# Two-layer mixer backbone on one core: latents' norms filled with gate products, norm sums reordered, unread products behind two broadcasts

## The chip, the cores and the metric

The kernel runs on one core of one Trainium2 chip. The metric is device time in microseconds (us) of one execution, the median of several. PE is TensorE (matrix products), DVE is VectorE, ACT is ScalarE, POOL is GpSimd; SP issues DMAs.

## The reference

Two layers work on 256 latent tokens and 256 context tokens of width 1024, in fp32. What matters of a layer:

```python
ux = rmsnorm(h, g_pre_mix[l]) * (1 + sc1x) + sh1x
yx, yc = token_mixers(ux, uc, ...)
h = h + ga1x * rmsnorm(yx, g_post_mix[l])
ux = rmsnorm(h, g_pre_ffn[l]) * (1 + sc2x) + sh2x
h = h + ga2x * rmsnorm(swiglu(ux, w_ffn_in[l], w_ffn_out[l]), g_post_ffn[l])

# in token_mixers: the latents of branch A, then four attention branches and their gates
q = heads(rmsnorm(p['a_cq'], g_a_q) @ w_a_uq, H_A)
kv = heads(rmsnorm(p['a_ckv'], g_a_kv) @ w_a_ukv, H_A)
up = jnp.einsum('btnw,nwd->btnd', o, w_branch)
g = jax.nn.sigmoid(gate_pre.reshape(up.shape))
return jnp.sum(g * up, axis=2) @ w_out
```

Branch A has 8 heads with low-rank queries and keys; B, C and D have 8 heads each in 4 pairs. Context tokens go through the same layer, except in the last one, where they only give keys and values.

## The kernel before

Activations stand with channels on partitions and tokens along the row, 512 columns in layer 0 and 256 for most of layer 1. Every fp32 product is made of three fp32r products (`three`: high x high, high x low, low x high), so each weight piece of 512 columns is first split: ACT copies the high part (L1323), DVE (L1508) or POOL (L1283) subtracts it to get the low part. A piece of four weight tiles gives 12 products on PE.

The order of all work is written out as a list of steps by `build_plan`, and every engine walks this list in order. There is no scheduler at run time: an engine that waits for a semaphore holds up everything behind it in its own queue. A layer has these stages.

1. The first projection (`group`, step `gmm`, 96 products in 8 pieces) makes the latents `ckv`, `cq` (two tiles) and the rotary key `kr` while `apply` still norms the input tile by tile (DVE L1632, ACT L1364 and L1369, DVE L1638 for the low part).
2. The latents' norms: `evac` and `evacsq` copy and square a product out of PSUM (ACT L1378, L1382), `stat` sums squares over partitions (PE L1864), then DVE, POOL and DVE make the reciprocal root and write it wide (`wide`, DVE L1584), `bcast` turns it over the partitions (PE L1923), `gn` multiplies (DVE L1654), `qks` stores high and low parts (ACT L1386, DVE L1673). `rot` and `rope` rotate `kr`. Then come the first head's projections and gates 0 and 1 (four pieces of 12 products).
3. Attention in slots. A slot (`run_slot`) has the scores of one item (`sc`, `sc2`), the row maximum (`mx`), the exponential (`ex`), the transposes (`tr`, PE L2002) and the value product (`pv`) of earlier items. Between them stand the projection steps of the next unit (a head of A, a pair of B, C or D), which `spread_over` deals out to the unit's slots, and filler: gate and up products of 12 products a piece, which `levels` and `Filler` spread by their cost. A unit's chain is: products, `evac`, for D also `stat` and `gain` (`bcast`, `gn`), `rotate` (PE L1932, then POOL and DVE), `store` (`qks`). The next unit's scores wait for that store.
4. `output` makes eight tiles of y; after each one ACT scales it into Y (`yev`, L1351), and squares y, Y and the product of Y with the residual are summed for the norms (`ysq`, `zsq`, `hz`, and the adds `yadd`, `zadd`, `hadd` on POOL, L1251).
5. `turnover` goes from one block to the next: the sums over partitions on PE (`sums` L1882 and L1886, `sums_rest` L1894), the first norm's root and broadcast, the `moment` of the new residual from the sums, its root and a second broadcast (both PE L1923), then `post` adds the normed y to the residual (DVE L1646, L1648) and `apply` feeds the next group of products. There are three turnovers, and a shorter end after the last block.

The lines that deal the projection steps out to slots, and the order in `apply`, are:

```python
for c, make in micro:
    at = min(slots - 1, int((gone + c / 2) * slots / whole))
    out[at].append((c, make))
    gone += c
```

```python
fill.todo = gate(0, 0) + gate(1, 0)
```

Of the kernel before, what the change touches and what calls it, by code (L numbers as in the profile page):

```python
# [29 lines left out]
P = 128  # L30
# [22 lines left out]
MOD_US = 1.2  # L53
AHEAD = 4
# [7 lines left out]
for _n, _w in (('ident', 128), ('ones', 1), ('power', 8), ('rotB', 128), ('rotA', 128), ('cosB', 256), ('sinB', 256),  # L62
# [21 lines left out]
RINGS = {'acc': 3, 'raw': 3, 'tmp': 2, 'fil': 2, 'gate': 8, 'Q': 2, 'K': 2, 'V': 2, 'S': 2, 'P': 2, 'Pn': 2, 'T': 1,  # L84
# [11 lines left out]
    'wide': ('stat_wide',), 'moment': ('moment_part', 'moment_part', 'moment_part', 'moment_part', 'moment_ready'),  # L96
# [12 lines left out]
    'tout': ('out_turned', 'out_copied'),  # L109
# [126 lines left out]
def build_plan():  # L236
# [28 lines left out]
    def apply(nm, l, which, n, first, posts=None):  # L265


        posts = posts or {}
        for kt in range(KT + 1):
            if kt < KT:  # L270
                p.take('tmp', ('ap', nm, kt), ('ap_full', (nm, kt)))
                p.take('fil', ('ap', nm, kt), ('ap_lo', (nm, kt)))
                p.step('apA', (nm, kt), l=l, which=which, n=n)
                for step in posts.get(kt, ()):
                    step()
            if kt:
                p.step('apB', (nm, kt - 1), n=n)
                p.step('gmm', (first, kt - 1))
# [4 lines left out]
    def turnover(nmo, nm, l, which, n, first):  # L283


        p.step('sums', nmo, n=n, what=('ysq', 'hz', 'zsq'))
# [4 lines left out]
        p.step('bcast', nmo, n=n)  # L291
        p.step('moment', nm, n=n)
# [3 lines left out]
        p.step('bcast', nm, n=n)  # L296
        post(nmo, 0, n)
# [25 lines left out]
    for l in range(DEPTH):  # L323
# [22 lines left out]


        for k, n in ((ckv, NTOK), (cq[0], nq), (cq[1], nq)):
            p.take('raw', k, ('op_hi', k), ('op_lo', k))
            p.take('fil', k, ('stat_sum', ckv if k == ckv else cq[1]))  # L350
            p.step('evac', k, rows=(0, P), n=n)
            p.step('evacsq', k, rows=(0, P), n=n)
            if k == ckv:
                norm_stat(ckv, [ckv], 1, KVL, NTOK, [('normed', ckv)])
                p.step('gn', ckv, bc=ckv, n=NTOK, g=(l, 82))
                p.step('qks', ckv, src='raw', rows=(0, P), n=NTOK, dst=('ckv', 0))
        norm_stat(cq[1], cq, 1, QL, nq, [('normed', cq[1])])
        p.take('raw', kr, ('op_hi', kr), ('op_lo', kr))
        p.step('evac', kr, rows=(0, DA), n=NTOK)
        for t, k in enumerate(cq):  # L360
            p.step('gn', k, bc=cq[1], n=nq, g=(l, 80 + t))
            p.step('qks', k, src='raw', rows=(0, P), n=nq, dst=('cq', t))
        p.take('acc', ('rot', kr), ('rope_sin', kr))
        p.step('rot', kr, rows=DA, t='A', normed=False)
        p.take('tmp', ('rope', kr), ('roped', kr))
        p.step('rope', kr, rows=DA, t='A')
        p.step('qks', kr, src='raw', rows=(NOPE, DA), n=NTOK, dst=('kr', 0))
# [90 lines left out]
        def projection(u):  # L458
# [41 lines left out]
            return [k0, k1, k_raw, q0, k_sum, q1, q_raw, k_norm, v0, q_sum, k_rot, v1, v_raw, q_norm, k_store, v_turn,  # L500
# [189 lines left out]
        fill.todo = gate(0, 0) + gate(1, 0)  # L690
# [20 lines left out]
        for n in range(4):  # L711
            a, b = n * per + 3 if n else 0, (n + 1) * per + 3
            if n == 0:
                fill.todo += [step for dt in range(2, KT) for step in gate(dt, 0)]
# [20 lines left out]
        def output(nmo, l, which, pieces_of, src, kts, need, ends=False):  # L735
# [3 lines left out]
            for dt in range(KT):  # L739
# [10 lines left out]
                p.step('yev', key, n=nq, l=l, which=which)  # L750
                for what in whats:
# [4 lines left out]
                    p.step(what, key, n=nq)  # L756
                for what in whats if 0 < dt < KT - 1 else ():
                    p.step(what[0] + 'add', key, n=nq)
# [50 lines left out]
    p.step('sums', nmf, n=SEQ, what=('ysq',))  # L809
    p.step('mstat', nmf, nh=1, dim=D, n=SEQ, after=('first_sums', nmf))  # L810
    p.step('wide', nmf, n=SEQ, of=1)
    p.take('bc', ('bc', nmf), ('post_scaled', (nmf, KT - 1)))
    p.step('bcast', nmf, n=SEQ)
    for kt in range(KT):
        post(nmf, kt, SEQ)
# [44 lines left out]
def build(nc, x, c, ctx, c_ctx, w_mod, b_mod, g_pre_mix, g_post_mix, g_pre_ffn, g_post_ffn, w_in, g_a_q, g_a_kv,  # L860
# [26 lines left out]
    with ExitStack() as es:  # L887
# [102 lines left out]
        def raw(key):  # L990
            at = RAW_AT + plan.slot['raw', key] * NTOK
            return Y[:, at:at + NTOK]
# [213 lines left out]
        def _(pool):  # L1206
            for kind, key, f in steps:
# [28 lines left out]
                elif kind == 'pow':  # L1236
                    m = f['n'] // P
                    pool.wait_ge(sem['moment_ready'], count['moment_ready', key])
                    pool.tensor_tensor(stat[:, 4, 0:m], stat[:, 3, 0:m], const('power')[:, 0:m],
                                       ALU.pow).then_inc(sem['stat_rstd'], 1)  # L1240
                elif kind in ('yadd', 'zadd', 'hadd'):
# [3 lines left out]
                    what, done = {'yadd': ('ysq', 'y_added'), 'zadd': ('zsq', 'z_added'), 'hadd': ('hz', 'h_added')}[kind]  # L1245
# [59 lines left out]
        def _(act):  # L1305
            for kind, key, f in steps:
# [63 lines left out]
                elif kind in ('evac', 'evacsq'):  # L1370
# [4 lines left out]
                    if kind == 'evac':  # L1375
                        for name, k_ in plan.freed['raw', key]:
# [93 lines left out]
        def _(dve):  # L1470
            for kind, key, f in steps:
# [92 lines left out]
                elif kind in ('stat', 'mstat'):  # L1564
# [10 lines left out]
                    if key == (0, 'pre_mix'):  # L1575
                        dve.tensor_copy(stat[:, 5, 0:m], sums[:, 0:m])
# [16 lines left out]
                elif kind == 'moment':  # L1593
# [4 lines left out]
                    done = count['moment_part', key] - 4  # L1598
# [6 lines left out]
                    dve.tensor_tensor(a, a, r, ALU.mult).then_inc(sem['moment_part'], 1)  # L1605
                    dve.wait_ge(sem['moment_part'], done + 3)
                    dve.tensor_tensor(h2, h2, a, ALU.add).then_inc(sem['moment_part'], 1)
# [503 lines left out]
```

## Time and profile before

| what | value |
|---|---|
| median of 3 runs | 1996.81 us (1995.76 to 1998.09) |
| the profiled execution | 1997.45 us |
| its span, first to last instruction | 1995.6 us |
| PE busy | 1832.3 us (92%) |
| DVE busy | 1222.5 us (61%) |
| ACT busy | 885.5 us (44%) |
| POOL busy | 681.6 us (34%) |
| mean granted PE clock | 0.961 |

The granted clock is 1.00 at 2.4 GHz and 0.50 at 1.2 GHz. Busy time of PE therefore holds time in which it worked at half pace; a stretch is read with its busy time and its granted clock together.

### The profile page before, as it was taken

What the parts mean: (1) busy time and instruction counts of PE and PEld (TensorE: products, weight loads), DVE (VectorE), ACT (ScalarE), POOL (GpSimd) and SP (SyncE); (2) the same over time, 40 slices, a digit from 0 to 9 for tenths busy, and PEclk for the clock granted to TensorE, in tenths of its full rate; (3) what the DMA queues carried; (4) which work ended last, traced back from release to release, by engine and by line L of the source; (5) the groups of instructions that cost most, each with busy time, mean ns of one, the idle gap of its engine ahead of it and who ended that gap; (6) DMA issues with size and microseconds to landing.
All of it is one profiled execution on the core that took longest, in us unless ns stands there. A gap on an engine that the chain in (4) does not pass through costs nothing. (4 is left out here: it accounts for less than half of the span.)

```text
span 1995.6 us, 31796 instructions
## 1 busy us (share of the span) xinstructions
PE 1832.3 (92%) x10675; PEld 1579.9 (79%) x10675; DVE 1222.5 (61%) x2381; ACT 885.5 (44%) x1918; POOL 681.6 (34%) x615
## 2 busy tenths in 40 slices
PE   7788899999998889989999999878999998989998
PEld 7666677778777768778888878767888887879997
DVE  6335565667775664667777775646554456776654
ACT  2435544444443444453222233456555544555453
POOL 6134434445443443541111112225335534351100
PEclk9979999999999999979999999789999999989998
DMA  7111223334433322424546664122343433436664
GB/s 292 55 37 43 60 78 87 85 107 121 116 96 85 80 64 68 134 83 134 148 140 186 198 197 118 46 57 66 97 110 97 117 91 89 113 117 175 185 180 122
DMA packets 381804, 223.15 MB, mean 112 GB/s; under 512 B 51607, under 2 KB 377549, under 8 KB 380621
## 3 DMA queue, kind: packets, MB, share of 16 engines
q1 hardware_dynamic: 379340, 217.97, 38.5%
q10 hardware_dynamic: 2304, 3.15, 0.6%
q8 instruction: 89, 1.46, 0.3%
q14 instruction: 71, 0.57, 0.1%
HBM read 217.92 MB, written 3.15 MB: 111 GB/s over the span
## 5 line engine op out<-in xcount | busy, mean ns | idle before, releaser
L1778 PE MATMUL bank<-Uhi,w_ring 128*128 128x512 f32 (+2 forms) x1664 | 592.5, 356 | 24.3 <-DVE Ulo L1638 15.6
L1780 PE MATMUL bank<-Uhi,w_ring 128*128 128x512 f32 (+2 forms) x1664 | 578.0, 347 | 0.0
L1779 PE MATMUL bank<-Ulo,w_ring 128*128 128x512 f32 (+2 forms) x1664 | 577.7, 347 | 0.0
L1508 DVE TENSOR_TENSOR w_ring<-load_ring,w_ring 128x512 fp32r<-128x512 f32 (+2 forms) x432 | 339.0, 802 | 173.2 <-ACT w_ring L1323 148.3
L1323 ACT ACTIVATE w_ring<-load_ring 128x512 fp32r<-128x512 f32 (+4 forms) x640 | 369.1, 602 | 90.9 <-PE bank L1780 70.3
L1778 PEld LDWEIGHTS bank<-Uhi,w_ring 128*128 128x128 f32 (+1 forms) x1664 | 319.8, 192 | 69.2 <-issue 22.4
L1780 PEld LDWEIGHTS bank<-Uhi,w_ring 128*128 128x128 f32 (+1 forms) x1664 | 319.0, 192 | 40.5
L1283 POOL TENSOR_TENSOR w_ring<-load_ring,w_ring 128x512 fp32r<-128x512 f32 (+3 forms) x208 | 249.2, 1201 | 290.6 <-issue 143.6
L1779 PEld LDWEIGHTS bank<-Ulo,w_ring 128*128 128x128 f32 (+1 forms) x1664 | 320.1, 192 | 34.9
L1778 PE MATMUL bank<-Z,w_ring 128*128 128x512 f32 (+2 forms) x784 | 273.7, 349 | 16.2 <-DVE Z L1673 6.1
L1779 PE MATMUL bank<-Z,w_ring 128*128 128x512 f32 (+2 forms) x784 | 269.1, 343 | 0.0
L1780 PE MATMUL bank<-Z,w_ring 128*128 128x512 f32 (+2 forms) x784 | 268.9, 343 | 0.0
L1271 POOL TENSOR_TENSOR Y<-Y,small 128x512 f32<-128x512 f32 x160 | 166.6, 1041 | 238.6 <-DVE small L1724 215.6
L1418 ACT ACTIVATE Y<-bank,small 128x512 f32<-128x512 f32 (+1 forms) x192 | 117.2, 612 | 146.2 <-DVE small L1707 145.9
L1778 PEld LDWEIGHTS bank<-Z,w_ring 128*128 128x128 f32 (+1 forms) x784 | 151.0, 193 | 36.6 <-issue 9.1
L1729 DVE TENSOR_TENSOR Z<-bank,Z 128x512 fp32r<-128x512 f32 x160 | 109.4, 684 | 99.7 <-ACT Z L1426 99.1
L1780 PEld LDWEIGHTS bank<-Z,w_ring 128*128 128x128 f32 (+1 forms) x784 | 151.1, 193 | 17.6
L1779 PEld LDWEIGHTS bank<-Z,w_ring 128*128 128x128 f32 (+1 forms) x784 | 151.3, 193 | 16.2 <-issue 0.3
L1300 POOL TENSOR_TENSOR Z<-fil,Z 128x512 fp32r<-128x512 f32 (+1 forms) x44 | 44.6, 1016 | 320.7 <-ACT Z L1460 320.7
L1778 PE MATMUL bank<-Z 128*64 128x256 f32 (+2 forms) x368 | 111.3, 303 | 25.1 <-DVE Z L1673 15.5
L1426 ACT ACTIVATE Z<-bank 128x512 fp32r<-128x512 f32 x160 | 95.0, 594 | 81.9 <-PE bank L2002 79.6
L1529 DVE SCALAR_TENSOR_TENSOR mod_sums<-mod_place,sc,mod_sums 128x256 f32<-128x256 f32 x224 | 123.6, 592 | 3.4 <-issue 0.3
(138 smaller groups left out, 2402.9 us busy)
## 6 DMA issues: line engine op xcount, KB each, us to landing
load_ring<-in_w_in SPq DMA_DIRECT2D x192, 256.0 KB, 3.0
load_ring<-in_w_ffn_in SPq DMA_DIRECT2D x160, 256.0 KB, 3.1
mod_ring<-in_w_mod SPq DMA_DIRECT2D x96, 256.0 KB, 3.1
load_ring<-in_w_ffn_out SPq DMA_DIRECT2D x80, 256.0 KB, 3.3
mod_place<-in_w_mod SPq DMA_DIRECT2D x64, 256.0 KB, 2.8
load_ring<-in_w_branch SPq DMA_DIRECT2D x64, 256.0 KB, 2.8
mod_w<-in_w_mod SPq DMA_DIRECT2D x8, 1024.0 KB, 13.6
load_ring<-in_w_in SPq DMA_DIRECT2D x64, 128.0 KB, 2.6
```

Source lines behind the costliest of these rows:

```text
L1271: pool.tensor_tensor(prob('Pn', key).rearrange("p (m k) -> p m k", m=m), prob('P', key).rearrange("p (m k) -> p m k", m=m), small[:, plan. ...
L1283: pool.tensor_tensor(w_ring[:, slot, 1, 0:sz], load_ring[:, plan.slot['load', key], 0:sz], w_ring[:, slot, 0, 0:sz].bitcast(F32), ALU.subt ...
L1300: pool.tensor_tensor(operand('hid', 1, key[1], n), fil[:, plan.slot['fil', ('ffn', key)], 0:n], operand('hid', 0, key[1], n).bitcast(F32), ...
L1323: act.activation(w_ring[:, plan.slot['w', key], 0, 0:sz], load_ring[:, plan.slot['load', key], 0:sz], ACT.Copy).then_inc(sem['w_hi'], 1)
L1418: ins = act.activation(prob('P', key)[:, a:b], s_bank(key)[:, a:b], ACT.Exp, bias=sm[:, 2 + i:3 + i], scale=scale_of(key), accum_out=sm[:, ...
L1426: act.activation(dst, src, ACT.Copy).then_inc(sem['pt_hi'], 1)
L1508: dve.tensor_tensor(w_ring[:, slot, 1, 0:sz], load_ring[:, plan.slot['load', key], 0:sz], w_ring[:, slot, 0, 0:sz].bitcast(F32), ALU.subtr ...
L1529: ins = dve.scalar_tensor_tensor(out=a, in0=w, scalar=by, in1=a, op0=ALU.mult, op1=ALU.add)
L1729: dve.tensor_tensor(dst, src, hi.bitcast(F32), ALU.subtract).then_inc(sem['pt_lo'], 1)
L1778: pe.matmul(dst, lhs[0], rhs[0], start=start, stop=False)
L1779: pe.matmul(dst, lhs[0], rhs[1], start=False, stop=False)
L1780: return pe.matmul(dst, lhs[1], rhs[0], start=False, stop=stop)
```

## The change

Five edits stand in the diff.

- Latents: the gates are put into the latents' norms. `AT_START` takes three gates (layer 0) or four (layer 1) instead of two, and of their six or eight pieces four or six are placed one at a time between the `stat`, `bcast` and `rot` steps. The evacuation of `kr` comes first and goes to a place of its own (`rawk`), so that the bank in which gates are made is free.
- Slots: `spread_over` gets fixed places for chains of five steps (B) and seven steps (D), and puts the others half a slot earlier; the order in D's first unit is altered.
- Sums: the last tile is squared before it is scaled (`ysq` before `yev`), `sums` holds only what the first norm needs, the rest goes to `sums_rest`; `hadd` moves from POOL to DVE; `moment` has four operations instead of five.
- `warm`: products of two constant tiles into bank 6, which nobody reads: four behind the first broadcast and six behind the second at each turnover, and four and four at the end. 38 in all.
- `apply`: the third `post` comes behind the first tile's products, not ahead of its low part, and so on for each tile.

```diff
+AT_START = (3, 4)
...
-        for kt in range(KT + 1):
-            if kt < KT:
-                p.take('tmp', ('ap', nm, kt), ('ap_full', (nm, kt)))
-                p.take('fil', ('ap', nm, kt), ('ap_lo', (nm, kt)))
-                p.step('apA', (nm, kt), l=l, which=which, n=n)
-                for step in posts.get(kt, ()):
-                    step()
-            if kt:
-                p.step('apB', (nm, kt - 1), n=n)
-                p.step('gmm', (first, kt - 1))
+        scaled(0)
+        for step in posts.get(0, ()):
+            step()
+        for kt in range(KT):
+            if kt + 1 < KT:
+                scaled(kt + 1)
+            p.step('apB', (nm, kt), n=n)
+            p.step('gmm', (first, kt))
+            for step in posts.get(kt + 1, ()):
+                step()
...
-        p.step('sums', nmo, n=n, what=('ysq', 'hz', 'zsq'))
+        p.step('sums', nmo, n=n)
         p.step('sums_rest', nmo, n=n, what=('hz', 'zsq'))
...
         p.step('bcast', nmo, n=n)
+        p.step('warm', nmo, times=4)
         p.step('moment', nm, n=n)
...
         p.step('bcast', nm, n=n)
+        p.step('warm', nm, times=6)
...
-            for c, make in micro:
-                at = min(slots - 1, int((gone + c / 2) * slots / whole))
-                out[at].append((c, make))
+            places = {5: (0, .3, .3, .6, .7), 7: (0, .2, .2, .4, .55, .75, .8)}.get(len(micro))
+            for i, (c, make) in enumerate(micro):
+                at = places[i] * slots if places else (gone + c / 2) * (slots - .5) / whole
+                out[min(slots - 1, int(at))].append((c, make))
                 gone += c
...
-        fill.todo = gate(0, 0) + gate(1, 0)
+        fill.todo = [step for dt in range(AT_START[l]) for step in gate(dt, 0)]
...
+        latent(ckv, NTOK)
+        p.take('rawk', kr, ('op_hi', kr), ('op_lo', kr))
+        p.step('evac', kr, rows=(0, DA), n=NTOK)
+        latent_sum(ckv, [ckv], KVL, NTOK)
+        latent(cq[0], nq)
+        fill.piece()
+        latent_rstd(ckv, NTOK)
+        latent(cq[1], nq)
+        latent_sum(cq[1], cq, QL, nq)
+        latent_store(ckv, ckv, NTOK, 82, ('ckv', 0))
+        fill.piece()
+        latent_rstd(cq[1], nq)
+        p.take('acc', ('rot', kr), ('rope_sin', kr))
+        p.step('rot', kr, rows=DA, t='A', normed=False)
+        fill.flush()
+        fill.piece()
+        if l:
+            fill.piece()
+            fill.flush()
+        for t, k in enumerate(cq):
+            latent_store(k, cq[1], nq, 80 + t, ('cq', t))
...
+        fill.piece()
+        if l:
+            fill.piece()
+        fill.flush()
...
+                elif kind == 'warm':
+
+                    for _ in range(f['times']):
+                        pe.matmul(bank[6][:, :], ident_r[:, :], mask_r[:, :], start=True, stop=True)
```

The order of PE's instructions behind the first group of layer 0, before. In all rows of this kind `bank` is PSUM, `C` the constants, `fil` the squares, `wide` the roots written wide, `Uhi` and `Ulo` the normed input, `Z` the attention's store, `w_ring` split weights; x4 is four in a row.

```order
L1864 MATMUL bank<-C,fil 128x1 x4
L1923 MATMUL bank<-C,wide 128x128 x4
L1864 MATMUL bank<-C,fil 128x1 x8
L1923 MATMUL bank<-C,wide 128x128 x4
L1932 MATMUL bank<-Y,C 96x256
L1778 MATMUL bank<-Z,w_ring 96x512
```

Now, from the end of the first gate piece (the row with L1828) on:

```order
L1828 MATMUL bank<-Uhi,w_ring 128x512
L1979 MATMUL bank<-C,wide 128x128 x4
L1912 MATMUL bank<-C,fil 128x1 x8
L1826 MATMUL bank<-Uhi,w_ring 128x512
L1827 MATMUL bank<-Ulo,w_ring 128x512
L1828 MATMUL bank<-Uhi,w_ring 128x512
```

A gate piece (12 products, of which one or three rows are shown) now stands behind the first sums and behind the second ones; two more follow the rotation of `kr`, ahead of the first head's products.

PE at the end of unit D0 of layer 0, before: the rotation (L1932) of unit D1's queries stands with only one item's transposes (L2002) between it and the scores (L1981) that need them.

```order
L1780 MATMUL bank<-Z 64x256
L1932 MATMUL bank<-Y,C 128x256
L2002 MATMUL bank<-C,Y 128x128 x4
L1981 MATMUL bank<-Z 128x512 x6
L1778 MATMUL bank<-Uhi,w_ring 128x512
```

Now, on PE at the end of the same unit: the rotation (L1988) follows the scores of the context item (L2037), and 50 rows stand between it and the next unit's scores.

```order
L1828 MATMUL bank<-Z,w_ring 128x512
L2058 MATMUL bank<-C,Y 128x128 x4
L2037 MATMUL bank<-Z 128x256 x12
L1988 MATMUL bank<-Y,C 128x256
L1826 MATMUL bank<-Z,w_ring 128x512
L1827 MATMUL bank<-Z,w_ring 128x512
```

So the rotation has moved ahead by filler products and by the scores of a whole item.

DVE at the turnover between the blocks of layer 0, before. L1646 and L1648 are a `post`, L1632 scales a tile, L1638 makes its low part `Ulo`, for which PE waits.

```order
L1632 TENSOR_TENSOR tmp<-H,bank 128x512
L1646 TENSOR_TENSOR Y<-Y,bank 128x512
L1648 TENSOR_TENSOR H<-H,Y 128x512
L1632 TENSOR_TENSOR tmp<-H,bank 128x512
L1646 TENSOR_TENSOR Y<-Y,bank 128x512
L1648 TENSOR_TENSOR H<-H,Y 128x512
L1638 TENSOR_TENSOR Ulo<-fil,Uhi 128x512
```

Now, on DVE at the same turnover:

```order
L1680 TENSOR_TENSOR tmp<-H,bank 128x512
L1694 TENSOR_TENSOR Y<-Y,bank 128x512
L1696 TENSOR_TENSOR H<-H,Y 128x512
L1680 TENSOR_TENSOR tmp<-H,bank 128x512
L1686 TENSOR_TENSOR Ulo<-fil,Uhi 128x512
L1694 TENSOR_TENSOR Y<-Y,bank 128x512
L1696 TENSOR_TENSOR H<-H,Y 128x512
```

The low part (L1686) has moved ahead of the second `post` pair (L1694, L1696).

## Rows read from the trace of the kernel before

**Rows 1.** The page, part 1: busy time of each engine, share of the span, instructions.

```profile
PE 1832.3 (92%) x10675; PEld 1579.9 (79%) x10675; DVE 1222.5 (61%) x2381; ACT 885.5 (44%) x1918; POOL 681.6 (34%) x615
```

**Rows 2.** Windows: stretch, its us, busy PE, PEld, DVE, ACT, POOL, granted clock, DMA share, GB/s.

```profile
90.00:129.50 39.50, 26.34 (x105) 21.43 (x106) 10.39 (x19) 12.35 (x24) 9.84 (x10) 0.70 0.10 26
129.50:250.00 120.50, 104.04 (x546) 83.04 (x546) 65.54 (x151) 68.05 (x162) 51.49 (x55) 0.93 0.20 50
580.00:780.00 200.00, 179.97 (x1001) 147.56 (x1001) 122.68 (x266) 82.14 (x189) 89.91 (x77) 0.96 0.28 76
862.00:864.80 2.80, 2.80 (x26) 2.76 (x25) 1.12 (x1) 2.36 (x5) 1.86 (x2) 1.00 0.00 0
862.20:904.30 42.10, 36.07 (x161) 31.09 (x160) 27.36 (x47) 20.68 (x37) 8.08 (x7) 0.76 0.30 88
865.00:885.30 20.30, 14.27 (x53) 12.58 (x53) 14.00 (x28) 7.10 (x13) 3.21 (x3) 0.50 0.33 101
904.30:1262.00 357.70, 353.65 (x1617) 293.50 (x1617) 248.21 (x461) 108.34 (x200) 57.46 (x41) 1.00 0.53 158
1300.60:1328.10 27.50, 16.97 (x92) 15.16 (x92) 11.78 (x23) 10.30 (x24) 4.31 (x6) 0.69 0.13 33
1328.10:1395.00 66.90, 60.05 (x398) 49.63 (x397) 44.23 (x107) 47.90 (x115) 31.73 (x37) 1.00 0.28 67
1600.00:1715.00 115.00, 103.51 (x771) 94.58 (x770) 69.62 (x153) 57.90 (x130) 45.34 (x47) 0.97 0.34 86
```

**Rows 3.** Timeline of PE, latents of layer 0: start us, us, instruction [idle before, releaser].

```profile
91.26 1.02 PE L1864 MATMUL bank<-C,fil 128*128 128x1 f32 x8 [1.27 <-ACT fil L1382]
94.18 2.05 PE L1923 MATMUL bank<-C,wide 128*128 128x128 f32 x8 [1.90 <-DVE wide L1584]
99.77 3.54 PE L1864 MATMUL bank<-C,fil 128*128 128x1 f32 x16 [3.54 <-ACT fil L1382]
105.21 2.04 PE L1923 MATMUL bank<-C,wide 128*128 128x128 f32 x8 [1.89 <-DVE wide L1584]
...
111.71 0.71 PE L1778 MATMUL bank<-Z,w_ring 128*96 128x512 f32 x1 [3.61 <-DVE Z L1673]
```

**Rows 4.** Timeline of PE: successive products of 512 columns at either clock.

```profile
112.22 0.63 PE L1779 MATMUL bank<-Z,w_ring 128*96 128x512 f32 x1
112.65 0.63 PE L1780 MATMUL bank<-Z,w_ring 128*96 128x512 f32 x1
...
126.14 0.39 PE L1778 MATMUL bank<-Uhi,w_ring 128*128 128x512 f32 x1
126.37 0.39 PE L1779 MATMUL bank<-Ulo,w_ring 128*128 128x512 f32 x1
```

**Rows 5.** Waits of PE, 129.5 to 250 us (branch A): us, times, longest us.

```profile
PE bank L1778 <- DVE Z L1673: 10.9, 7, 2.7
PE bank L1932 <- ACT Y L1378: 5.4, 7, 1.1
```

**Rows 6.** Waits of PE, 250 to 415 us (branch B).

```profile
PE bank L1932 <- ACT Y L1378: 3.8, 3, 1.3
```

**Rows 7.** Waits of PE, 415 to 580 us (branch C).

```profile
PE bank L1778 <- DVE Z L1729: 8.3, 5, 3.1
```

**Rows 8.** Waits of PE, layer 1, 1395 to 1600 us (branches B and C).

```profile
PE bank L1932 <- ACT Y L1378: 3.2, 3, 1.1
```

**Rows 9.** Timeline of PE, turnover inside layer 0.

```profile
869.77 2.05 PE L1923 MATMUL bank<-C,wide 128*128 128x128 f32 x8
872.60 2.05 PE L1923 MATMUL bank<-C,wide 128*128 128x128 f32 x8 [0.77 <-DVE wide L1591]
879.90 0.76 PE L1778 MATMUL bank<-Uhi,w_ring 128*128 128x512 f32 x1 [5.26 <-DVE Ulo L1638]
```

**Rows 10.** Timeline of DVE, the same turnover.

```profile
877.53 0.68 DVE L1646 TENSOR_TENSOR Y<-Y,bank 128x512 f32<-128x512 f32 x1
878.25 0.69 DVE L1648 TENSOR_TENSOR H<-H,Y 128x512 f32<-128x512 f32 x1
```

More of the change, by code:

```diff
@@ L713, in build_plan @@
             if n == 0:
-                fill.todo += [step for dt in range(2, KT) for step in gate(dt, 0)]
+                fill.todo += [step for dt in range(AT_START[l], KT) for step in gate(dt, 0)]
             else:
@@ L756, in output @@
                     p.step(what, key, n=nq)
+                    if dt == KT - 1 and what == 'ysq':
+                        p.step('yev', key, n=nq, l=l, which=which)
                 for what in whats if 0 < dt < KT - 1 else ():
@@ L808, in build_plan @@
                {j: [('hid_lo', (l, min(4 * j + 3, FT - 1)))] for j in range(-(-FT // 4))}, ends=last)
-    p.step('sums', nmf, n=SEQ, what=('ysq',))
+    p.step('sums', nmf, n=SEQ)
     p.step('mstat', nmf, nh=1, dim=D, n=SEQ, after=('first_sums', nmf))
+    p.step('warm', (nmf, 0), times=4)
     p.step('wide', nmf, n=SEQ, of=1)
@@ L813, in build_plan @@
     p.step('bcast', nmf, n=SEQ)
+    p.step('warm', (nmf, 1), times=4)
     for kt in range(KT):
@@ L1621, in _ @@
                                       ALU.mult).then_inc(sem['hz_done'], 1)
+                elif kind == 'hadd':
+                    nm, dt = key
+                    n = f['n']
+                    dve.wait_ge(sem['hz_done'], count['hz_done', key])
+                    if dt > 1:
+                        dve.wait_ge(sem['h_added'], count['h_added', (nm, dt - 1)])
+                    a = sum_place('hz', (nm, 0))[:, 0:n]
+                    dve.tensor_tensor(a, a, sum_place('hz', key)[:, 0:n], ALU.add).then_inc(sem['h_added'], 1)
                 elif kind == 'apA':
@@ L1876, in _ @@
                 elif kind == 'sums':
-                    for j, what in enumerate(f['what']):
-                        done = {'ysq': 'y_added', 'hz': 'h_added', 'zsq': 'z_added'}[what]
-                        pe.wait_ge(sem[done], count[done, (key, KT - 2)])
-                        for tt in range(f['n'] // P):
-                            pe.matmul(sums_at(j, tt), sum_place(what, (key, 0))[:, tt * P:(tt + 1) * P], const('ones'),
-                                      start=j < 2 and tt == 0, stop=False, skip_group_check=True)
+                    pe.wait_ge(sem['y_added'], count['y_added', (key, KT - 2)])
+                    for tt in range(f['n'] // P):
+                        pe.matmul(sums_at(0, tt), sum_place('ysq', (key, 0))[:, tt * P:(tt + 1) * P], const('ones'),
+                                  start=tt == 0, stop=False, skip_group_check=True)
                     pe.wait_ge(sem['ysq_done'], count['ysq_done', (key, KT - 1)])
@@ L1888, in _ @@
                     ins.then_inc(sem['first_sums'], 1)
+                elif kind == 'warm':
+                    for _ in range(f['times']):
+                        pe.matmul(bank[6][:, :], ident_r[:, :], mask_r[:, :], start=True, stop=True)
                 elif kind == 'sums_rest':
+                    for j, what in enumerate(f['what']):
+                        done = what[0] + '_added'
+                        pe.wait_ge(sem[done], count[done, (key, KT - 2)])
+                        for tt in range(f['n'] // P):
+                            pe.matmul(sums_at(1 + j, tt), sum_place(what, (key, 0))[:, tt * P:(tt + 1) * P], const('ones'),
+                                      start=j == 0 and tt == 0, stop=False, skip_group_check=True)
                     for j, what in enumerate(f['what']):
```

74 lines of the change are left out of this document (38 added, 36 removed).

## The prediction

> **What bounds the kernel now.** The engines' busy times come first: PE 1832.3 us of a span of 1995.6, DVE far behind at 61% [rows 1]. So a change pays in one of two ways: it takes away some of PE's 163 us without work (1995.6 - 1832.3), or it gives back pace that PE lost at the low clock. The mean clock of 0.961 puts that at 0.039 x 1995.6 = 78 us at most. Second, the windows by stage say where both lie [rows 2]. The output and ffn stages are all but full (353.65 of 357.70 us, clock 1.00) and have nothing to give. The latents have 13 us of idle in 39.5, at clock 0.70; branch A of layer 0 16.5 us at 0.93; branch D 20 us at 0.96; the turnover 6 us at 0.76. Third, the timeline and the waits say what ends the idle there: a chain through ACT, DVE and POOL, with nothing ready behind it in PE's own queue [rows 3, 5, 9]. Does the order of the queue put work of the right length there, and is that work ready?
>
> I count savings against the profiled execution, 1997.45 us (0.6 above the median).
>
> **Latents, layer 0: 16.5.** Two rows of products start 0.43 us apart at the low clock and 0.23 at the high one [rows 4], so a piece of 12 takes 2.7 us at the high clock (12 x 0.227) and 5.1 at the low. Before, 39.5 us held four pieces [rows 2]. In the change it holds six. Its length, if PE never waits long: six pieces 16.4; sums 1.0 and, at the high clock, half of 3.54 (taken as 2.0); two broadcasts of 2.05, of which I take 1.25 each, between half and the whole; rotations and turning of v 1.6; the first head's nine products 2.1; the wait of 1.3 ahead of the first sums, which nothing fills [rows 3]. That is 27. The two added pieces were paid later before, at 5.5, so the saving is 39.5 + 5.5 - 27 = 18. The cover fits: the first piece starts about 92.3 and would end at 95.0, where the first broadcast could start at 94.18; after the second broadcast the first head's operands need 4.4 us (107.25 to 111.71) [rows 3], and two pieces are 5.5. I take 1.5 off for one low-clock spell more, leaving 16.5. Bounds: nothing of the clock comes back (13 us of idle only, less 2), 11; all of it, 18.
>
> **Latents, layer 1: 11.5.** Gate pieces have half the columns there, so 1.4 us each. Eight instead of four stand in a stretch of 27.5 with 10.5 of idle at clock 0.69 [rows 2]. The same working gives 20.2 us with the four added ones (5.5): 27.5 + 5.5 - 20.2 = 12.8, less 1.3. Bounds 7 and 13.
>
> **Turnovers: 4.7.** In the first, PE's first product waits 5.26 us for the low part [rows 9], and a `post` pair of about 0.7 and 0.7, paced at 1.3, stands ahead of it on DVE [rows 10]; the change puts it behind. The shorter `moment` saves a little more. Against it, the four unread products run at the low clock, 4 x 0.43 = 1.7 us, where PE had only 0.77 us free: the second broadcast goes out some 0.9 late. The six behind it (2.6) lie in the 5.26. The product thus starts about 0.9 earlier. The group behind it runs at the low clock until 885.3 [rows 2]; if the unread products raise it by the time it starts, twelve products cost 2.7 us instead of 5.1. I take 2.5 in all; ends -0.9 and 3.5. The other two turnovers get 0.8 and 0.7, as DVE's chain paces them whatever PE does, and the end 0.7. The moved sums are worth nothing: the same 48 products stand ahead of the first broadcast. `hadd` on DVE costs nothing, because DVE is idle for 110 of 358 us in the output and ffn stages [rows 2]; without that cover it would add 0.7 a tile.
>
> **Attention slots: 43.** I take idle first. Branch A, layer 0: 16.5 us idle [rows 2], of it 10.9 for the store of the next head and 5.4 for the copy ahead of the rotation [rows 5]. Half a slot earlier moves the store out of the way, but the rotation's copy now queues on ACT behind the exponential: 4 net. Branch B: three rotations wait 3.8 [rows 6], and the fixed places put scores between; 3.8, and 3.2 in layer 1 [rows 8]. Branch D, layer 0: 20 us [rows 2], since copy, rotation and store all stand in the unit's last slot; the order shows 50 rows between rotation and scores now, and I take 14.5. Branch A, layer 1: 5.5 of 6.85; branch D, layer 1: 7.5 of 11.5 [rows 2]. Sum 38.5. The clock gives more: PE's busy time in these stretches would shrink by 104.04 x 0.07 = 7.3, 179.97 x 0.04 = 7.2 and 103.51 x 0.03 = 3.1 if it never fell [rows 2]. The spells stand where PE idles; I take half of the first and 80% of the others, 11.9 in all. Off the 50.4 I take 15%, since each unit's products moved ahead also leave work further back bare: branch C, whose chain is unfilled in places, waits 8.3 us for the stores of values [rows 7]. That leaves 43. Bounds: 15 and 55.
>
> The Trainium skill ("TensorE: Matmul & The Clock Gate", section "What's actually happening") says that the clock's ramp costs under 1% of a typical span and need not be modelled. By it the clock's part of all savings would be capped near 20 us; the measured mean of 0.961 says 3.9% here, so rows are followed.
>
> **Sum.** 16.5 + 11.5 + 4.7 + 43 = 75.7; 1997.45 - 75.7 = 1921.75, and 0.6 less for the median: **1921**.
>
> **Rivals.**
> - The slots only move waits (0.13). A wait on the store is exchanged for one on the copy or on values, as [rows 7] shows it where chains are spread evenly. Against it: D's chain is so bunched that any spreading helps. The slots then give 0: 1997.5 - 32.7 = 1964 or so.
> - The pieces in the latents come too late (0.07): their weights must be split by ACT and DVE, which also carry the norms' chain; PE waits for them in place of the root. Half of the 28 goes: 1935.
> - The clock stays up from the latents to the end (0.08). With the long idle gone no gap falls in attention or the turnovers, and the terms that I halved come whole: another 10 us, 1911. For it: most low spells follow idle time. Against it: the clock fell at 864.9, right behind 2.80 us in which PE was busy all the time, and stayed at 0.50 to 885.3 [rows 2].
> - It gets slower (0.04). Place: branch A of both layers. With products dealt half a slot earlier its last slots have only small products and waits for the copy, and the clock falls there. At half clock the 164 us of busy time in the two branches (104.04 + 60.05, [rows 2]) double. The 16.5 + 6.85 = 23 us of idle there absorb a part, so if all of it runs low the loss is 141, against 75.7 saved: 2062. It decides from more than half of that time at the low clock.
>
> [...]
>
> **How the numbers follow.** The forecast has 0.68, the rivals 0.13, 0.07, 0.08 and 0.04. The forecast's own range is 1903 to 1938, from the bounds of the terms taken together and not all at one end (all at their low ends would save about 11 + 7 + 1 + 15 = 34, all at the high ends 18 + 13 + 6 + 55 = 92). The range for 8 in 10 must reach into the first rival without holding it whole: 1900 to 1957. Measurements of this kernel tell changes of about 0.2%, 4 us, from none. Faster by more has the forecast and three rivals, 0.96, less 0.01 for cases close to none: 0.95; within, 0.01; slower, 0.04.
>
> **What would show it.** Right: the stretch from the first group to the first scores falls from 39.5 to about 27 us with 72 gate products in it, at a clock over 0.85; the wait of the products for the store (10.9 in branch A) halves; branch D is idle for 5 to 8 us instead of 20; the first product of the turnover's group waits near 3.5 us instead of 5.26 and the low spell there is shorter. Wrong: branch A's waits for the copy above 15 us; DVE or ACT named before the latents' pieces; the low spell from 864.9 as long as before; the mean clock still under 0.97. The whole fails if PE's idle time stays above 130 us.

## The result, and the profile after

The changed kernel takes 1984.5 us, median of 6 runs (1980.31 to 1995.71), against 1997.33 us (1995.76 to 1998.41) for the kernel before: a ratio of 0.9947, interval 0.9926 to 0.9968. It is faster by 12.8 us at the medians, where 76 were forecast, and the time lies outside the range. Its profiled execution took 1985.07 us. Its six runs lie 15 us apart; the granted clock of the slowest is 0.966, of the others 0.969 to 0.972.

The page of the changed kernel, part 1 (against [rows 1]):

```profile
PE 1834.7 (93%) x10713; PEld 1584.7 (80%) x10713; DVE 1229.0 (62%) x2396; ACT 883.0 (45%) x1918; POOL 654.7 (33%) x597
```

PE has the same work and the 38 unread products, and the span fell by 12.3 us to 1983.3: its idle time went from 163 to 149 us.

Windows of the changed kernel at the stages of [rows 2], in the same columns; the bounds are placed by the same instructions: latents, A, D, turnover, output and ffn of layer 0; then latents, A, B with C, and D of layer 1.

```profile
90.00:118.40 28.40, 26.00 (x134) 20.75 (x132) 10.77 (x18) 13.01 (x26) 11.01 (x12) 1.00 0.18 46
118.40:240.60 122.20, 104.14 (x547) 84.56 (x546) 63.10 (x152) 67.66 (x162) 50.95 (x55) 0.92 0.20 50
564.90:753.50 188.60, 172.91 (x977) 142.34 (x977) 124.67 (x263) 78.56 (x182) 87.75 (x76) 0.96 0.28 76
837.40:882.00 44.60, 38.84 (x172) 32.79 (x171) 26.26 (x46) 20.56 (x37) 7.77 (x6) 0.85 0.27 83
882.00:1239.60 357.60, 353.55 (x1619) 293.44 (x1617) 250.94 (x467) 108.33 (x200) 48.21 (x35) 1.00 0.53 158
1282.50:1307.70 25.20, 18.75 (x141) 17.13 (x141) 12.37 (x25) 12.87 (x32) 6.01 (x8) 1.00 0.25 60
1307.70:1379.30 71.60, 59.38 (x359) 49.81 (x360) 41.93 (x104) 45.41 (x110) 30.35 (x37) 0.93 0.22 52
1379.30:1594.00 214.70, 199.97 (x1360) 178.04 (x1359) 105.37 (x239) 107.13 (x243) 89.87 (x83) 0.98 0.40 100
1593.80:1705.60 111.80, 103.01 (x782) 94.05 (x781) 69.40 (x154) 58.91 (x132) 46.95 (x47) 0.98 0.36 90
```

Four things stand in them. The latents of layer 0 are close to the forecast's 27: 39.5 has become 28.4 at clock 1.00, with two more pieces in it. Branch A got longer in both layers (120.5 to 122.2, 66.9 to 71.6), and so did B with C in layer 1: 214.7 us, and before, in the same columns:

```profile
1395.00:1600.00 205.00, 196.89 (x1371) 175.10 (x1370) 106.25 (x238) 107.64 (x245) 90.25 (x83) 1.00 0.42 106
```

The turnover inside layer 0 is 2.5 us longer than before, though the low spell is shorter. The output and ffn stages didn't move, with `hadd` on DVE (x461 to x467): that was free.

### The profile page after: what moved, and what is told of

Its sections match the earlier page's. It is cut to its first block and busy times, and to the rows that moved or that the text cites. A ratio compares the mean times of both kernels' runs of the same rounds, so it can differ in the third digit from the quotient of the medians.

```text
span 1983.3 us, 31864 instructions
## 1 busy us (share of the span) xinstructions
PE 1834.7 (93%) x10713; PEld 1584.7 (80%) x10713; DVE 1229.0 (62%) x2396; ACT 883.0 (45%) x1918; POOL 654.7 (33%) x597
## 3 DMA queue, kind: packets, MB, share of 16 engines
q1 hardware_dynamic: 379340, 217.97, 38.6%
## 5 line engine op out<-in xcount | busy, mean ns | idle before, releaser
L1828 PE MATMUL bank<-Uhi,w_ring 128*128 128x512 f32 (+2 forms) x1664 | 577.7, 347 | 0.0
L1550 DVE TENSOR_TENSOR w_ring<-load_ring,w_ring 128x512 fp32r<-128x512 f32 (+2 forms) x432 | 333.2, 789 | 163.8 <-ACT w_ring L1365 133.1
L1828 PEld LDWEIGHTS bank<-Uhi,w_ring 128*128 128x128 f32 (+1 forms) x1664 | 319.2, 192 | 40.5
L1828 PE MATMUL bank<-Z,w_ring 128*128 128x512 f32 (+2 forms) x784 | 267.7, 341 | 0.0
L1460 ACT ACTIVATE Y<-bank,small 128x512 f32<-128x512 f32 (+1 forms) x192 | 117.3, 613 | 173.2 <-DVE small L1755 173.2
L1828 PEld LDWEIGHTS bank<-Z,w_ring 128*128 128x128 f32 (+1 forms) x784 | 150.4, 192 | 17.2
L1826 PE MATMUL bank<-Z 128*64 128x256 f32 (+2 forms) x368 | 113.3, 308 | 21.4 <-DVE Z L1777 10.9
```

Of the source, the lines that this page charges most:

```text
L1460: ins = act.activation(prob('P', key)[:, a:b], s_bank(key)[:, a:b], ACT.Exp, bias=sm[:, 2 + i:3 + i], scale=scale_of(key), accum_out=sm[:, ...
L1550: dve.tensor_tensor(w_ring[:, slot, 1, 0:sz], load_ring[:, plan.slot['load', key], 0:sz], w_ring[:, slot, 0, 0:sz].bitcast(F32), ALU.subtr ...
L1826: pe.matmul(dst, lhs[0], rhs[0], start=start, stop=False)
L1828: return pe.matmul(dst, lhs[1], rhs[0], start=False, stop=stop)
```

## Where the time went in the trace

The timeline of PE, latents of layer 0, changed kernel (the rows between are gate products):

```profile
92.35 1.02 PE L1912 MATMUL bank<-C,fil 128*128 128x1 f32 x8 [1.26 <-ACT fil L1424]
...
96.36 1.13 PE L1979 MATMUL bank<-C,wide 128*128 128x128 f32 x8
97.33 1.84 PE L1912 MATMUL bank<-C,fil 128*128 128x1 f32 x16
...
101.88 1.05 PE L1979 MATMUL bank<-C,wide 128*128 128x128 f32 x8
```

The waits of 1.90, 3.54 and 1.89 of [rows 3] are gone, and the sixteen sums (3.54 to 1.84 us) and the broadcasts (2.05 to 1.13 and 1.05) take half as long.

The waits of PE in branch A of layer 0 (118.4 to 240.6 us), changed kernel: us, times, longest us.

```profile
PE bank L1988 <- ACT Y L1420: 8.2, 4, 2.2
PE bank L1826 <- DVE Z L1721: 5.3, 5, 1.8
PE bank L2058 <- POOL Y L1313: 4.6, 2, 2.3
```

Against [rows 5] the wait for the store has halved, from 10.9 to 5.3, and the copy ahead of the rotation has grown from 5.4 to 8.2; a third wait of 4.6 is new, of transposes for the probabilities that POOL scales. 16.3 us of waits have become 18.1: this is the first rival (waits are only moved), in this branch.

The timeline of PE, turnover inside layer 0, changed kernel; L1938 are the unread products:

```profile
845.71 2.05 PE L1979 MATMUL bank<-C,wide 128*128 128x128 f32 x8
847.42 2.05 PE L1938 MATMUL bank<-mask_r,ident_r 128*128 128x512 f32 x4
849.27 1.32 PE L1979 MATMUL bank<-C,wide 128*128 128x128 f32 x8
850.35 1.63 PE L1938 MATMUL bank<-mask_r,ident_r 128*128 128x512 f32 x6
854.43 0.48 PE L1826 MATMUL bank<-Uhi,w_ring 128*128 128x512 f32 x1 [2.45 <-DVE Ulo L1686]
...
861.67 0.50 PE L1826 MATMUL bank<-Uhi,w_ring 128*128 128x512 f32 x1 [1.50 <-DVE Ulo L1686]
...
869.22 0.50 PE L1826 MATMUL bank<-Uhi,w_ring 128*128 128x512 f32 x1 [1.81 <-DVE Ulo L1686]
```

The clock is up at the first product, as hoped, and the wait ahead of it fell from 5.26 to 2.45. But PE now waits again and again inside the group. The timeline of DVE there says why:

```profile
855.91 0.69 DVE L1686 TENSOR_TENSOR Ulo<-fil,Uhi 128x512 fp32r<-128x512 f32 x1
858.40 0.69 DVE L1550 TENSOR_TENSOR w_ring<-load_ring,w_ring 128x512 fp32r<-128x512 f32 x1 [1.80 <-issue]
859.01 0.68 DVE L1694 TENSOR_TENSOR Y<-Y,bank 128x512 f32<-128x512 f32 x1
859.73 0.69 DVE L1696 TENSOR_TENSOR H<-H,Y 128x512 f32<-128x512 f32 x1
```

Behind the low part stands the split of the next weight piece (L1550), and DVE idles 1.8 us ahead of it. The row names no releaser ("issue"); the timeline of ACT has the copy of the high part, which the split subtracts, ending just before, at 858.32:

```profile
857.70 0.62 ACT L1365 ACTIVATE w_ring<-load_ring 128x512 fp32r<-128x512 f32 x1
```

Only then does DVE do the `post`, which could have covered part of that wait. Over the whole group DVE waits 8.2 us ahead of such splits (854 to 882 us); before it was 6.2 (879.9 to 904.5), so the old order covered a part and not all. I measured each turnover from its first sum on PE to the end of the 96th and last product of the group. Before, the first product stands 17.7, 18.1 and 12.0 us behind the first sum and the 96th ends at 42.3, 38.6 and 28.0. After, the first stands at 17.0, 16.8 and 10.5 and the 96th ends at 44.6, 42.9 and 28.4. So the change wins 3.5 us at the first product and is 7.1 behind at the end of the groups.

## The experiments

Each kernel ran 4 to 12 times. The ratio is that to the kernel before in the same job, with its interval; the kernel before read 1997.1 to 1998.0 in all of them.

| run | us | ratio | interval |
|---|---|---|---|
| the changed kernel | 1984.50 | 0.9947 | 0.9926 to 0.9968 |
| e1_apply_undone | 1982.04 | 0.9918 | 0.9902 to 0.9934 |
| e2_slots_undone | 1989.01 | 0.9959 | 0.9944 to 0.9974 |
| e3_latents_undone | 2008.38 | 1.0047 | 1.0030 to 1.0064 |
| e4_no_unread | 1991.80 | 0.9964 | 0.9950 to 0.9978 |
| e5_places_only | 1959.00 | 0.9815 | 0.9797 to 0.9833 |
| e6_post_first | 1984.74 | 0.9942 | 0.9927 to 0.9958 |
| e7_places_post_first | 1950.63 | 0.9778 | 0.9760 to 0.9796 |
| e8_places_alone | 1975.86 | 0.9900 | 0.9883 to 0.9917 |
| e9b_latents_alone | 1986.95 | 0.9957 | 0.9942 to 0.9971 |
| e10b_half_slot_in_c | 1977.02 | 0.9897 | 0.9881 to 0.9912 |
| e11b_places_no_unread | 1964.26 | 0.9835 | 0.9819 to 0.9852 |
| e12b_places_old_apply | 1958.60 | 0.9806 | 0.9792 to 0.9821 |

**One part undone.** e1_apply_undone has the old order in `apply`:

```diff
-            p.step('gmm', (first, kt))
-            for step in posts.get(kt + 1, ()):
-                step()
...
+                for step in posts.get(kt, ()):
+                    step()
+            if kt:
+                p.step('apB', (nm, kt - 1), n=n)
+                p.step('gmm', (first, kt - 1))
```

> The changed kernel with the old order in apply (each post ahead of the low part again), all else kept. Theory: behind the new order DVE meets the split of a weight piece with nothing left to do and idles 1.8 us for ACT's high part, at five tiles, then still has the post to do; the groups behind the turnovers are longer by 3 and 5.7 us in the traces (order of work aligned). Undone, the time falls by 5 to 10 us, to about 1977, although the first product waits longer. Rival, the forecast's own term: the new order saves 2.5 to 4 us, and undone the time rises to 1987 to 1989.

The direction is the theory's: undoing it is no loss, and the 96th product ends at 42.0, 37.7 and 27.3. The medians differ by 2.5 us, the ratios by 5.8, and the two intervals overlap, so the size isn't settled by this run. In its trace DVE waits 5.1 us ahead of the splits of the first group, against 8.2.

e2_slots_undone has the spread of before, and the old order in D's first unit:

```diff
-            places = {5: (0, .3, .3, .6, .7), 7: (0, .2, .2, .4, .55, .75, .8)}.get(len(micro))
...
+                at = min(slots - 1, int((gone + c / 2) * slots / whole))
```

> The changed kernel with the old spread over the slots (no fixed places, no half slot earlier, old order in D's first unit). Theory: branches B and D gain some 10 + 9 us in layer 0 and 3 + 9 in layer 1 by the fixed places, branches A and C lose 2 + 5 and 6 + 14 by the half slot earlier: net almost nothing, 1980 to 1995 us. Rival, the forecast's term of 43: about 2025 us.

1989.0: by the medians all edits of the slots together are worth 4.5 us here, by the ratios 2.4, with overlapping intervals, where the forecast had 43. This is the term that failed.

e3_latents_undone has the old block for the latents and `gate(0, 0) + gate(1, 0)` at the start:

```diff
-        fill.todo = [step for dt in range(AT_START[l]) for step in gate(dt, 0)]
+        fill.todo = gate(0, 0) + gate(1, 0)
...
```

> The changed kernel with the old latents (two gates at the start, norms unfilled). Theory: the added pieces came out of branch A, where they had covered waits, so that part of the gain is given back: latents 17 + 9 us, less 5 to 6 in each layer's branch A, leaving 12 to 16: 1997 to 2001 us. Rival, the forecast's term of 28 is whole: 2012 us.

2008.4: the latents are worth 24 us inside the change by the medians (20 by the ratios), nearer to the forecast's 28 than to my 12 to 16. Without them the rest of the change is slower than the kernel before.

e4_no_unread leaves out the four `warm` steps:

```diff
-        p.step('warm', nmo, times=4)
...
-        p.step('warm', nm, times=6)
...
```

> The changed kernel without the 38 unread products. Theory: they cut the low-clock spell at a turnover from 20.5 to 10.2 us, but the group behind is paced by DVE with the new apply order, so little of it reaches the time: 1984 to 1990 us. Rival 1, the clock is worth it all the same (about 5 us at each of two turnovers): 1993 or more. Rival 2, they only delay the second broadcast by 0.8 us each: 1982.

7.3 us slower at the medians, a value between theory and rival, but 3.4 by the ratios, and the two intervals overlap: the size isn't settled. The second rival, that they cost time, finds no support. The traces don't put the gain at the turnovers. The low spell behind the first broadcast is 20.5 us long again instead of 10.2, yet the group takes 27.1 us, with the unread products 27.6. And most of the difference between the traces can't be put down to them. Up to the first turnover the two kernels are the same, instruction for instruction, and this trace is already 5.1 us behind there, of 7.2 in all; 3.8 of them stand in branch C of layer 0, where the low clock holds for 20.5 us instead of 10.2. Behind that point the latents of layer 1 take 1.7 us more and branch C 2.3, and the turnovers 1.8 less.

**The slots taken apart.** e5_places_only keeps the fixed places of B's and D's chains and takes the half slot back from all the others:

```diff
-                at = places[i] * slots if places else (gone + c / 2) * (slots - .5) / whole
+                at = places[i] * slots if places else (gone + c / 2) * slots / whole
```

> The changed kernel with the fixed places of B's and D's chains kept, and all other chains (those of A and C) spread as before, without the half slot. Theory: the half slot is what loses. By the aligned traces branch C loses 5 us in layer 0 and 14 in layer 1 by it, and branch A a few: 1960 to 1968 us. Rival, the clock: what one stage gains another loses to spells of the low clock that move about, and the time stays within 5 us of the changed kernel's 1984.5.

1959.0, just below the theory's 1960 to 1968, and the intervals are far apart: **the half slot costs 25 us**. Against e2, whose slots are all as before, the fixed places and the order in D's first unit are worth 30 us inside the change (29 by the ratios). e10b_half_slot_in_c puts it back for C alone:

```diff
-                at = places[i] * slots if places else (gone + c / 2) * (slots - .5) / whole
+                at = places[i] * slots if places else (gone + c / 2) * (slots - early) / whole
...
-                micros[at_item:at_item + len(mine)] = spread_over(micro, len(mine))
+                micros[at_item:at_item + len(mine)] = spread_over(micro, len(mine), .5 * (u2[1] == 'C'))
```

> The kernel with places only, with the half slot put back for branch C's chains alone. Theory: of the 25 us that the half slot costs, C holds the larger part (7 us in layer 0 and 12 in layer 1 by the aligned traces), by its turns of v that stand right behind their products while ACT's copy is still to come: 1975 to 1980 us. Rival: the loss is branch A's, and the time stays at 1959 to 1964.

1977.0: C holds 18 of the 25 us by the medians (16 of 26 by the ratios); the rest belongs to the chains of A and to the long first chains of B and D, which this pair of runs doesn't tell apart. In the traces branch A of layer 1 takes 88.8 us with the half slot and 81.3 without. The waits of PE in branch C of layer 1 show where C loses, in four kernels. Before (1500 to 1612 us):

```profile
PE bank L1940 <- ACT Y L1378: 3.1, 3, 1.5
```

Changed kernel (1484 to 1606 us):

```profile
PE bank L1996 <- ACT Y L1420: 11.5, 4, 3.5
```

Half slot in C alone (1476 to 1594 us):

```profile
PE bank L1996 <- ACT Y L1420: 10.7, 4, 3.0
```

Places only (1472 to 1580 us):

```profile
PE bank L1996 <- ACT Y L1420: 2.5, 2, 1.7
```

L1940 and L1996 are the same instruction, the turn of v, and wait for the copy out of PSUM. The timeline of ACT in the changed kernel tells what the copy itself waits for; PE's turn is the row below.

```profile
1514.91 0.58 ACT L1468 ACTIVATE Z<-bank 128x512 fp32r<-128x512 f32 x1
1515.39 0.62 ACT L1365 ACTIVATE w_ring<-load_ring 128x512 fp32r<-128x512 f32 x1
1517.03 0.69 ACT L1460 ACTIVATE Y<-bank,small 128x512 f32<-128x512 f32 x1 [1.03 <-DVE small L1755]
1517.62 0.19 ACT L1460 ACTIVATION_READ_ACCUMULATOR Y<-bank,small 128x1 f32 x1
1517.71 0.59 ACT L1420 ACTIVATE Y<-bank 128x512 f32<-128x512 f32 x1
```

```profile
1518.44 0.73 PE L1996 MATMUL bank<-C,Y 128*128 128x128 f32 x4 [3.54 <-ACT Y L1420]
```

The copy (L1420) stands in ACT's queue behind the exponential of another item (L1460), which waits for DVE's maximum. PE, which has the turn next in its own queue, stands idle meanwhile.

e8_places_alone is the kernel before with the fixed places and the order of D's first unit:

```diff
-                at = min(slots - 1, int((gone + c / 2) * slots / whole))
...
+            places = {5: (0, .3, .3, .6, .7), 7: (0, .2, .2, .4, .55, .75, .8)}.get(len(micro))
...
+                at = places[i] * slots if places else (gone + c / 2) * slots / whole
...
```

> The kernel before with the fixed places of B's and D's chains and the new order in D's first unit, nothing else. Theory: 10 us in B and 8 in D of layer 0, 3 and 9 in layer 1: 1967 to 1972 us. The forecast's terms for the same stages were 3.8, 14.5, 3.2 and 7.5 of idle and 8.3 of clock, less 15 per cent: 1966. Rival, the clock: below 10 us of gain, 1988.

1975.9, faster by about 21 us (22 by the medians, 20 by the ratio), less than the theory's 25 to 30. The first three units of D in layer 0, in windows between the first transposes of the first and the fourth, before and with the places alone:

```profile
638.00:756.40 118.40, 105.12 (x592) 86.49 (x591) 73.69 (x166) 48.70 (x113) 50.19 (x43) 0.94 0.27 73
```

```profile
636.20:745.70 109.50, 102.73 (x592) 84.80 (x591) 79.85 (x170) 47.99 (x112) 51.52 (x45) 0.97 0.30 79
```

The same PE work in 8.9 us less: 6.5 of idle and the rest by the clock. Against that stands branch A of layer 0. Its own chains stand as before; only gate pieces among them moved to later slots, and one more falls into it. In this trace it takes 147.5 us instead of 137.9, at clock 0.91 instead of 0.94 (the row of the kernel before stands below, first under "The latents"):

```profile
137.90:285.40 147.50, 127.78 (x656) 102.14 (x655) 75.46 (x175) 75.42 (x180) 56.67 (x60) 0.91 0.20 50
```

**The latents.** e9b_latents_alone is the kernel before with the new block for the latents and its place for `kr`:

```diff
-        fill.todo = gate(0, 0) + gate(1, 0)
+        fill.todo = [step for dt in range(AT_START[l]) for step in gate(dt, 0)]
...
```

> The kernel before with the filled latents and the larger start (three and four gates), nothing else. Theory: the latents save 17 us in layer 0 and 9 in layer 1, but the two and four pieces taken out of branch A had covered waits there, so that its length stays: 1982 to 1988 us. Rival, the forecast's term of 28 (pieces paid later at their full price before): 1969.

1987.0: 10 us by the medians, inside the theory's range. Windows over branch A from its first transposes to B's, layer 0 and layer 1; before:

```profile
138.50:276.40 137.90, 119.71 (x643) 96.37 (x642) 76.62 (x174) 74.99 (x179) 56.80 (x60) 0.94 0.20 51
1336.90:1419.70 82.80, 74.83 (x490) 62.49 (x489) 49.45 (x117) 52.01 (x123) 38.13 (x42) 1.00 0.30 70
```

Latents alone:

```profile
126.40:270.30 143.90, 120.52 (x631) 97.32 (x630) 76.52 (x178) 74.50 (x179) 54.66 (x58) 0.89 0.19 47
1324.90:1404.80 79.90, 70.82 (x455) 58.16 (x454) 48.74 (x118) 50.17 (x121) 37.42 (x43) 1.00 0.27 64
```

In layer 1 the branch lost 35 products and 2.9 us: nearly their price, so they had hardly been needed as cover. In layer 0 it lost 12 products and became 6.0 us longer. 5.2 of that is idle time (143.90 - 120.52 against 137.90 - 119.71), and it stands at one wait, of the head's products for the store, 10.9 us before [rows 5]; latents alone, 126.4 to 270.3 us:

```profile
PE bank L1808 <- DVE Z L1703: 15.9, 7, 4.4
```

So the pieces that were taken out had been cover here, as the theory said. The rest is the clock, 0.89 instead of 0.94: PE is busy 0.8 us longer with 12 products (2.7 us) less, 3.5 us of lost pace. The clock of this branch differs between traces without the latents' edit too (0.91 in e8), so that its fall is due to the latents isn't shown.

**The turnovers, and a better version.** e6_post_first puts the `post` ahead of the group's step, and with it ahead of the split in DVE's queue:

```diff
-            p.step('gmm', (first, kt))
             for step in posts.get(kt + 1, ()):
                 step()
+            p.step('gmm', (first, kt))
```

> The changed kernel with each post between the low part and the weight split (behind the low part still, but ahead of the group's step, so ahead of the split on DVE). Theory: the post then fills the 1.8 us in which DVE waits for ACT's high part; the first product stays at 17.0 us behind the first sums and the 96th ends at 41 instead of 44.6 in layer 0, 38 instead of 42.9 in layer 1: 1975 us. Rival: DVE's sum of work paces the group whatever the order, 1984.

The mechanism came as expected; the timeline of DVE in this kernel:

```profile
860.59 0.69 DVE L1686 TENSOR_TENSOR Ulo<-fil,Uhi 128x512 fp32r<-128x512 f32 x1
861.19 0.68 DVE L1694 TENSOR_TENSOR Y<-Y,bank 128x512 f32<-128x512 f32 x1
861.91 0.69 DVE L1696 TENSOR_TENSOR H<-H,Y 128x512 f32<-128x512 f32 x1
863.43 0.69 DVE L1550 TENSOR_TENSOR w_ring<-load_ring,w_ring 128x512 fp32r<-128x512 f32 x1 [0.83 <-ACT w_ring L1365]
```

The 96th product ends at 41.7, 40.6 and 26.8 us behind the first sum instead of 44.6, 42.9 and 28.4, 6.8 us in sum, so the rival (DVE's sum of work paces the group whatever the order) doesn't hold. The time did not fall. Up to the first turnover this kernel is the changed kernel instruction for instruction, and its trace is 4.8 us behind there, 3.7 of it in branch C, where the low clock holds for 20.5 us instead of 10.2. In e7_places_post_first the same edit stands on the kernel with places only:

> The two edits before together. Theory: the gains add, 1952 to 1960 us, and this beats both kernels. Rival, the clock: 1975 or more.

1950.6, 8.4 us below the places alone, and faster than both kernels of this case, by 34 us and by some 46. Its trace and that of e5 run alike to within 0.3 us through A and B of layer 0; it gains 2.0 us in C, where the low clock holds for 6.8 us instead of 13.7, and 5.1 from the first turnover to the first unit of layer 1, a stretch with two of the turnovers. Of the 9.6 us between the two traces 2.7 lie ahead of the first turnover, where the kernels are the same; the edit can have given the other 7.

e12b_places_old_apply has e5's slots and e1's `apply`:

> The kernel with places only, with the old order in apply. Theory: the 96th product behind a turnover comes earlier by 2.6, 5.2 and 1.1 us than in the changed kernel, 8 to 9 in all: 1949 to 1953 us, about as with the post ahead of the split (1950.6). Rival: only the 2.5 us that undoing it in the changed kernel gave: 1956.

1958.6: a miss, no gain that can be measured. Windows of the turnover between the layers, from the first sum to the first product and over the group behind it. Places only:

```profile
1237.30:1252.50 15.20, 12.95 (x76) 11.96 (x74) 8.33 (x18) 5.09 (x10) 3.04 (x3) 0.78 0.06 15
1252.50:1278.50 26.00, 18.70 (x96) 13.59 (x96) 18.73 (x28) 14.42 (x27) 2.14 (x2) 1.00 0.27 65
```

With the old apply:

```profile
1235.40:1253.70 18.30, 14.60 (x75) 13.55 (x73) 9.54 (x20) 5.84 (x11) 3.04 (x3) 0.72 0.05 13
1253.70:1275.80 22.10, 19.62 (x96) 14.98 (x96) 16.83 (x26) 13.68 (x25) 2.17 (x2) 0.92 0.30 76
```

The group is 3.9 us shorter, and the way to it 3.1 longer: the low part is later by the `post` ahead of it, and the clock was lower. Over the three turnovers the 96th product ends 2.0, 0.8 and 1.3 us earlier, counted from the first sum, instead of the 8 to 9 in all that I had expected, and the latents of layer 1 take 2.3 us more in this trace.

e11b_places_no_unread is e5 without the `warm` steps:

> The kernel with places only, without the 38 unread products. Theory: the group behind each turnover is paced by DVE, so the spell of the low clock that they shorten costs little: 1957 to 1962 us, as with them. Rival: they are worth about 7 us, as the pair of runs of the changed kernel with and without them read: 1966.

1964.3, 5.3 us more (4.0 by the ratios, and the intervals overlap): the rival was nearer. Both pairs of kernels point the same way, 5 to 7 us by the medians and 3 to 4 by the ratios, and in neither do the turnovers' groups show more than a part of it. Here 1.5 of the 6.3 us between the traces lie ahead of the first unread product.

## Why the prediction was wrong, point by point

- **By stage**, each branch measured from its first transposes to the next one's, the traces before and after differ so: latents -16.4 us (12.5 and 3.8), branches B and D together -29.5, A +6.9, C +19.0, turnovers +7.1. The rest is under 1.
- **What bounds the kernel** was right: all gains and losses lie in idle time and low clock, none in the output and ffn stages.
- **Latents, layer 0 (16.5):** right where it happens, 39.5 - 28.4 + 5.5 = 16.6. **Layer 1 (11.5):** 27.5 - 25.2 + 5.5 = 7.8; the first head's products wait 2.1 us for their weights' split on POOL, as the second rival had it. What I left out is branch A of layer 0, which lost the cover: alone the two are worth 10 us (e9b). Inside the change they are worth 20 to 24 (e3), and the traces show where the two cases part: alone branch A of layer 0 becomes 6.0 us longer, inside the change 4.6 shorter, and branch C of layer 0 3.8 shorter. Why is open.
- **Turnovers (4.7):** the step that failed is "the change puts it behind", priced by the first product alone. In the following tiles the `post` had been covering a part of DVE's wait for the weight split. 3.5 us were won at the first products, 7.1 lost by the end of the groups; e1 and e6 show it, whose groups end 8.9 and 6.8 us earlier with the old order and with the same `post` ahead of the split. The moved sums and `hadd` at nothing stand. The unread products delay the second broadcast by 0.74 us (it starts 1.51 behind the end of the first instead of 0.77; forecast 0.9) and raise the clock, as forecast; the group that was to profit by it is paced by DVE. The whole term is small: by e1 the order costs 2.5 to 5.8 us.
- **Slots (43):** here the forecast failed. Its part for the fixed places was right: some 32 of the 43 belong to B and D with their part of the clock, less 15%, and the measured worth is 21 alone (e8), 30 inside the change (e5 against e2) and 29.5 in the stages of the traces. The step that failed is the half slot's: it was booked as a gain in branch A, 4 and 5.5 us of idle and half of 7.3 of clock, with "I take 15%", 7.6 us, off the whole term for work further back and branch C named as the place. It costs 25 us, most of them in C (e5, e10b), and branch A got longer. I had written for branch A that the copy queues behind the exponential, and did not ask the same of C's turn of v, which waits for its copy.
- **Rivals:** the first had the slots right, 0 where 4.5 or less was measured, but not for its reason, since a gain and a loss of the same size stand in them; and it kept the other terms whole and so came to 1964. The fourth, that branch A loses its clock, was right in sign, 0.93 to 0.92 in layer 0 and 1.00 to 0.93 in layer 1 [rows 2], and far from its point of decision. The second is seen only in layer 1, with 2.1 us. The third is out: the clock fell 25 times in the changed kernel, 18 before. The Trainium skill ("TensorE: Matmul & The Clock Gate", section "Why this matters for your kernels") warns of long idle gaps between bursts of products, behind which the clock falls. Here such gaps aren't the only cause: branch A of layer 1 has no wait over 1.7 us in the changed kernel, and its clock is 0.93.
- **The range** rested on all terms standing at once; that the slots give nothing was given 0.13, a slower kernel 0.04. Nor do the parts add up: taken out of the changed kernel one at a time they are worth 24, 4.5, -2.5 and 7.3 us by the medians (latents, slots, order of `apply`, unread products), and all together 12.8.

## What to carry to other kernels

Before work is issued earlier, ask of every instruction of the chain which engine makes its input, and what that engine has in its queue ahead of it: in this kernel the early products did no harm that a run shows, the early reader of a copy did. An instruction that is moved off a critical chain was perhaps part of the cover of the next wait on its own engine; follow the change through the whole loop and not to the first product alone. When several spacings change in one edit, time each class of chains by itself: here one was worth +21 and another -25.

## What had not been expected of the hardware

Spells of the low clock come also where PE only waits in short pieces (branch A of layer 1: longest wait 0.9 us and clock 1.00 before, 1.7 and 0.93 after). They also move without any edit: the changed kernel, e1, e4 and e6 have the same instructions up to the first turnover, and their traces reach it at 837.4, 840.5, 842.5 and 842.2 us. So a difference of under some 5 us between the spans of two traces isn't yet an effect, and edits of a few us don't add up in single pairs: the old order of `apply` gave 2.5 and 0.4 us (e1, e12b), the `post` ahead of the split 0 and 8.4 (e6, e7). Whether the unread products are worth the 5 to 7 us of the medians, where the groups behind them hardly gain, stays open.
